# Hybrid attention and delta-rule layer: the gate row's partition sum from a high and a low part, and new orders for all five queues

## The reference

```python
mod = silu(c) @ ada_w[l] + ada_b[l]
shift, scale, gate = split(mod, 3)
h = rmsnorm(x, pre_norm_w) * (1 + scale) + shift
proj = h @ w_in[l]
o_moba = moba_attention(mq, mk, mv) * silu(mg)      # one block of 256: causal softmax
o_dn = rmsnorm(gated_delta_rule(dq, dk, dv, g, beta), dn_norm_w) * silu(dz)
y = concat([o_moba, o_dn]) @ w_out[l]
x = x + gate * rmsnorm(y, post_norm_w)
```

## Time and profile before

| | us |
|---|---|
| median of 3 runs (200.59 to 201.94) | 201.45 |
| the profiled execution's own time | 201.38 |
| its span, first to last instruction | 199.2 |
| TensorE busy in it | 185.7 |
| VectorE, ScalarE, GpSimd busy | 138.4, 104.1, 83.4 |
| transfers | 38.43 MB, mean 193 GB/s |

### The profile page before, as it was taken

One profiled execution on the slowest core, in us unless ns is written; L12 is line 12 of the kernel. 1 busy time (PEld: TensorE's weight loads), 2 busy tenths in 40 slices (PEclk: granted clock), 3 DMA queues, 4 the chain that ended last, 5 costly groups with the idle time before them and its releaser, 6 DMA issues.

```text
span 199.2 us, 4716 instructions
## 1 busy us (share of the span) xinstructions
PE 185.7 (93%) x1898; PEld 170.3 (86%) x1898; DVE 138.4 (69%) x326; ACT 104.1 (52%) x201; POOL 83.4 (42%) x46
## 2 busy tenths in 40 slices
PE   7999779999999989999999999997999999899970
PEld 6897769999999989988989999896999987588850
DVE  0638989463079988979878646746989399837364
ACT  2835445636398869396553226385234548337230
POOL 2037709795969616928065003974000220504000
PEclk9988999999999999999999999999999999999998
DMA  5999999999106530197308400062029357910022
GB/s 211 394 403 404 409 396 407 400 406 408 42 0 207 175 147 0 44 396 305 105 3 273 151 3 3 3 212 106 3 74 412 151 205 223 359 59 0 3 107 105
DMA packets 11527, 38.43 MB, mean 193 GB/s; under 512 B 1393, under 2 KB 1521, under 8 KB 10994
## 3 DMA queue, kind: packets, MB, share of 16 engines
q1 hardware_dynamic: 11362, 37.61, 50.6%
q10 hardware_dynamic: 144, 0.52, 0.7%
HBM read 37.08 MB, written 1.05 MB: 191 GB/s over the span
## 4 chain that ended last, share of the span: by engine, by line
PE 51%; DVE 28%; DMA 8%; ACT 6%; issue 3%; POOL 1%; DVEq 0%; SPq 0%; ACTq 0%; POOLq 0%
PE bank L1337 11%; PE bank L1338 10%; PE bank L1339 10%; DVE cv L951 7%; DVE accg L1139 5%; DMA raw<-in_w_out 4%; PE bank L1348 4%; DVE bank L926 3%; DMA outb<-in_post_norm_w 3%; PE bank L1547 3%; PE bank L1558 3%; PE bank L1535 2%; DVE pr L1114 2%; ACT whi L544 1%; DVE ssq L1003 1%
## 5 line engine op out<-in xcount | busy, mean ns | idle before, releaser
L471 POOL TENSOR_TENSOR wlo<-raw,whi 128x1024 fp32r<-128x1024 f32 (+1 forms) x25 | 57.4, 2317 | 66.7 <-ACT whi L544 66.7
L1337 PE MATMUL bank<-hhi,whi 128*128 128x256 f32 x224 | 65.3, 292 | 3.0 <-DVE hlo L895 2.1
L1338 PE MATMUL bank<-hhi,wlo 128*128 128x256 f32 x224 | 63.6, 284 | 0.0
L1339 PE MATMUL bank<-hlo,whi 128*128 128x256 f32 x224 | 63.5, 283 | 0.0
L1337 PEld LDWEIGHTS bank<-hhi,whi 128*128 128x128 f32 x224 | 43.1, 193 | 5.2 <-DVE hlo L895 2.9
L1338 PEld LDWEIGHTS bank<-hhi,wlo 128*128 128x128 f32 x224 | 43.2, 193 | 0.0
L1339 PEld LDWEIGHTS bank<-hlo,whi 128*128 128x128 f32 x224 | 43.1, 193 | 0.0
L544 ACT ACTIVATE whi<-raw 128x1024 fp32r<-128x1024 f32 (+1 forms) x33 | 33.0, 1026 | 10.6 <-PE bank L1339 7.5
L951 DVE SCALAR_TENSOR_TENSOR cv<-bank,convh,cv 128x255 f32<-128x255 f32 (+2 forms) x36 | 17.0, 481 | 8.6 <-ACT cv L608 7.6
L926 DVE SCALAR_TENSOR_TENSOR bank<-ada,sml,bank 128x512 f32<-128x512 f32 (+1 forms) x24 | 16.5, 687 | 0.7
L485 POOL TENSOR_TENSOR rot<-rot,cst 128x512 f32<-128x512 f32 x4 | 4.4, 1091 | 22.3 <-DVE rot L1081 20.4
(11 more groups left out here) (203 smaller groups left out, 359.0 us busy)
## 6 DMA issues: line engine op xcount, KB each, us to landing
raw<-in_w_rest SPq DMA_DIRECT2D x20, 512.0 KB, 5.1
ada<-in_ada SPq DMA_DIRECT2D x12, 512.0 KB, 8.7
ada<-in_gate_w SPq DMA_DIRECT2D x4, 1024.0 KB, 8.3
raw<-in_w_out SPq DMA_DIRECT2D x8, 512.0 KB, 6.2
ada<-in_ada SPq DMA_DIRECT2D x8, 256.0 KB, 6.1
raw<-in_w_qkv SPq DMA_DIRECT2D x5, 384.0 KB, 7.7
qkvs<-in_w_qkv SPq DMA_DIRECT2D x4, 384.0 KB, 9.2
cv<-in_w_qkv SPq DMA_DIRECT2D x4, 384.0 KB, 13.6
```

The lines of the kernel that those rows point to most:

```text
L471: pool.tensor_tensor(split_u(wlo, n), raw_u(n), split_u(whi, n).bitcast(F32), ALU.subtract).then_inc(lo_done, 1)
L1337: pe.matmul(out, a[0][ia], b[0][ib], start=start, stop=False, skip_group_check=skip)
L1338: pe.matmul(out, a[1][ia], b[0][ib], start=False, stop=False, skip_group_check=skip)
L1339: return pe.matmul(out, a[0][ia], b[1][ib], start=False, stop=stop, skip_group_check=skip)
```

## The change

Four things. `gate_sum` multiplies rounded parts in place of float32: ScalarE rounds the ones (once) and a half of `accg` to `g_hi` (`gate_hi`), VectorE forms `g_lo = accg - g_hi` (`gate_lo`), and TensorE adds two products of 512 columns. The parts lie over `rot`, so `gate_hi(0)` waits for the last `rope`, and `gate_hi(1)` for `gate_sum(0)`. Of the low parts of the weights, units 34, 35, 37, 38 and 41 go from VectorE to GpSimd, and 28 from GpSimd to VectorE. And the lists of calls of all five queues stand in another order.

```diff
-        DVE_LO = (21, 34, 35, 37, 38, 41, 42, 43)
+        DVE_LO = (21, 28, 42, 43)
...
+            def gate_hi(i):
+                act.wait_ge(gate_acc, NK * (i + 1))
+                if i == 0:
+                    act.wait_ge(rope_done, 4)
+                    act.activation(g_ones, ones[:, :], ACT.Copy)
+                else:
+                    act.wait_ge(gate_ready, 1)
+                act.activation(g_hi, accg[:, i * 512:(i + 1) * 512], ACT.Copy).then_inc(gate_hi_done, 1)
...
+            def gate_lo(i):
+                dve.wait_ge(gate_hi_done, i + 1)
+                dve.tensor_tensor(g_lo, accg[:, i * 512:(i + 1) * 512], g_hi.bitcast(F32), ALU.subtract).then_inc(gate_split, 1)
...
             def gate_sum(i):
-                pe.wait_ge(gate_acc, NK * (i + 1))
+                pe.wait_ge(gate_split, i + 1)
...
-                pe.matmul(bank[6][:, :], ones[:, :], accg[:, i * 512:(i + 1) * 512], start=True, stop=True).then_inc(gate_ready, 1)
+                pe.matmul(bank[6][:, :], g_ones, g_hi, start=True, stop=False)
+                pe.matmul(bank[6][:, :], g_ones, g_lo, start=False, stop=True).then_inc(gate_ready, 1)
...
+            load_gates()
             load_front()
             load_ada(0, 0, 2)
             load_ada(0, 2, 4)
+            load_gate_bias()
             load_unit(0)
-            load_ada(1, 2, 4)
+            load_unit(1)
             load_ada(1, 0, 2)
             load_unit(2)
-            load_unit(1)
+            load_ada(1, 2, 4)
...
             qkv_products(8)
+            mod(4)
             qkv_products(9)
-            mod(4)
...
             scores(1)
-            half(10)
-            half(11)
             t_turn(1, 0)
+            t_turn(1, 1)
             z_products(1, 0)
-            t_turn(1, 1)
```

More of the change, by code:

```diff
@@ L143, in build @@
         sb("hold_qkvs", [P, NQKV * S + 1024])
-        rot = sb("rot", [P, 3, 512])
+        with ExitStack() as e:
+            rot = sb("rot", [P, 3, 512], into=e)
+        with ExitStack() as e:
+            gsplit = sb("gsplit", [P, 3, 512], F32R, into=e)
+        sb("hold_rot", [P, 3 * 512])
         pr, pT = sb("pr", [P, 2, 384]), sb("pT", [P, 2, 384])
@@ L1233, in _ @@
             gates_in()
-            rope(0)
             conv_silu(0)
             conv_silu(1)
+            rope(0)
             gates_out()
@@ L1262, in _ @@
             gated_heads(0)
+            v_tokens(1)
             mask_z(0, 0)
-            maxima(1)
-            v_tokens(1)
             mask_z(0, 1)
-            rope(2)
-            normalise(1)
             mask_z(1, 0)
@@ L1271, in _ @@
             merge(1, 0)
-            q_decayed(0)
+            rope(2)
             merge(1, 1)
+            maxima(1)
             mask_z(2, 0)
@@ L1277, in _ @@
             merge(2, 1)
+            mask_z(3, 0)
+            lo(28)
             q_decayed(1)
-            mask_z(3, 0)
+            normalise(1)
             merge(3, 0)
@@ L1285, in _ @@
             rope(3)
-            heads_lo(0)
+            gate_sums(0, 0, 4)
             mask_z(4, 1)
             mask_z(5, 0)
-            gated_heads(1)
             merge(4, 1)
             merge(5, 0)
+            gated_heads(1)
+            mask_z(5, 1)
             maxima(2)
+            gate_sums(0, 4, 8)
+            heads_lo(0)
             normalise(2)
-            heads_lo(1)
-            mask_z(5, 1)
-            lo(34)
+            gate_sums(1, 0, 4)
             merge(5, 1)
-            gate_sums(0, 0, 4)
-            gate_sums(0, 4, 8)
             gate(1)
+            gate(2)
             gated_heads(2)
-            lo(35)
             state_update(0)
             maxima(3)
-            gate_sums(1, 0, 4)
+            gate_sums(1, 4, 8)
             normalise(3)
-            heads_lo(2)
-            gate(2)
             state_update(1)
             gate(3)
-            gate_sums(1, 4, 8)
+            gate_lo(0)
+            o_sums(0)
             state_update(2)
-            o_sums(0)
+            o_scale(0)
+            heads_lo(1)
+            heads_lo(2)
             gated_heads(3)
-            o_scale(0)
-            lo(37)
-            lo(38)
+            gate_rows(0)
+            gate_lo(1)
             o_sums(1)
-            gate_rows(0)
+            gate_rows(1)
+            heads_lo(3)
             o_scale(1)
-            heads_lo(3)
             o_gate(0)
             o_gate(1)
-            gate_rows(1)
             dn_lo(0)
-            lo(41)
+            dn_lo(1)
             lo(42)
             lo(43)
-            dn_lo(1)
             finish(0)
@@ L1764, in _ @@
             half(7)
+            rows(0)
             scores(0)
-            rows(0)
             half(8)
@@ L1786, in _ @@
             x_products(1, 1)
+            t_turn(2, 0)
             z_products(2, 0)
-            t_turn(2, 0)
+            half(10)
             t_turn(2, 1)
@@ L1792, in _ @@
             x_products(2, 1)
-            t_turn(3, 0)
             z_products(3, 0)
             z_products(3, 1)
+            t_turn(3, 0)
+            half(11)
             x_products(3, 0)
@@ L1802, in _ @@
             t_turn(4, 1)
+            p_turn(1)
             t_turn(5, 0)
@@ L1805, in _ @@
             z_products(5, 0)
-            p_turn(1)
+            pv(1)
             half(12)
-            pv(1)
             x_products(4, 1)
             x_products(5, 0)
+            z_products(5, 1)
+            t_turn(5, 1)
             scores(2)
@@ L1814, in _ @@
             half(14)
-            p_turn(2)
-            t_turn(5, 1)
-            z_products(5, 1)
-            u_products(0)
-            x_products(5, 1)
-            pv(2)
-            w_products(1)
             half(15)
             half(16)
+            half(17)
+            x_products(5, 1)
+            u_products(0)
+            p_turn(2)
+            w_products(1)
+            pv(2)
             state_products(0)
             scores(3)
-            half(17)
+            half(18)
             vnew_products(1)
-            half(18)
             half(19)
             state_products(1)
+            p_turn(3)
             qk_products(0)
```

161 lines of the change are left out of this document (83 added, 78 removed).

## The result

The changed kernel takes 205.59 us (median of 4 runs, 205.31 to 207.54), the kernel before beside it 201.14 (4 runs, 200.59 to 201.94). The ratio is 1.024, with a 95% interval of 1.016 to 1.031: slower by about 4.5 us, and 2.2 above the range that was forecast. Medians here are of all runs; the ratios leave out runs of over 1.5% above the fastest of the same kernel. The profiled execution took 205.31 us, its span is 203.2, 4.0 more than before.

What follows compares the result with a forecast made beforehand. The prediction took TensorE's work and waits, plus what lies before its first and after its last product, as the bound. Terms -0.9 - 0.3 - 1.2 + 1.3 + 0.6 = -0.5 against 201.38 gave 200.9 us, range 198.6 to 203.4.

Steps and rivals of the forecast that it cites:

- the inverse's levels: half(10) and half(11) move out of the first level's front; hand-over gaps and normalise(1) perhaps caught: +0.6 us, ends 0.1 and 2.7.
- the thin cover: First level of the inverse, no half covering hand-overs: four gaps of 0.05 to 0.15 us, 0.3 in sum.
- the chance of the collision: normalise(1) may be caught by lo(29), making merge(3,0) late and t_turn(4,0) wait 0.4 us, taken at even chances.
- Gate sum, -0.9: Two rounded products replace one float32 product on TensorE, saving 0.47 us twice; subtractions and roundings lie beside other work.
- Wait before the second gate sum, -0.3: The 0.5 us wait for gate_rows(0) goes, gate_lo(1) arrives about 0.2 late: -0.3 us together; ends -0.5 and +0.7.
- `p_turn(2)`, -1.2: Five halves (14.4 us) now stand ahead, covering VectorE's 11.3 us chain, so TensorE's wait goes: -1.2 us.
- `p_turn(3)`, +1.3: Reached earlier, while lo(36) on GpSimd catches normalise(3) after its first multiplication: 8.2 against 7.0 us; ends 0 and 1.8.
- The front, 0: load_gates and load_gate_bias go first, 0.43 us issue each, covered by TensorE's dummy products and turns of x: zero, else +0.4.
- The clock in the earlier trace: TensorE's granted clock before the change was read as full in all slices but three of the first four and the last.
- 10% by way of the gate sums: Third rival: lo(35) reaches into gate_sums(1, 4, 8) and all behind moves, up to 2.4 us: +1.9, 203.3 us, chance 10%.
- the rivals: No new wait, 198.9 us (26%); gate's low parts caught, 204.3 (9%); gate sums caught, 203.3 (10%); transfers late, 202.2 (7%).
- Those with a collision: Rivals where GpSimd's low parts hold VectorE: gate_lo subtractions caught, 204.3 us (9%); gate sums caught, 203.3 us (10%).

Runs made afterwards that it cites:

- The kernel with the three edits: Changed kernel with load_gates behind load_unit(4), normalise(1) ahead of q_decayed(1) and lo(28), merge(5,1) ahead of gate_sums(1,0,4): 199.62 us, ratio 0.993.
- 6 dummies: Gate weights later, normalise(1) first and merge ahead, with 6 dummy products of TensorE ahead of mod_direct(2) in place of 8: 199.25 us (5 runs).
- that edit alone in the kernel before: Kernel before with only load_gates (gate weights, 32 KB in 128 packets) moved ahead of load_front: 202.26 us, ratio 1.005.

## Why the prediction was wrong

The step that failed is that of the inverse's levels: "At even chances with rounding up: +0.6 us; ends 0.1 and 2.7, one full low part on top". It cost 5.1. Three things were mis-sized there or left out.

- *How many low parts.* I saw that `normalise(1)` may be caught by `lo(29)` and stopped there. `hi(29)` and `hi(30)` stand next to each other on ScalarE, so GpSimd has two low parts without a gap, and an operation of VectorE that missed the first start waits for both (4.82 us). The bound had to be two: 2.4 more than mine. The wait of TensorE was 2.54 where I wrote 0.4.
- *What follows a wait.* I counted waits as their own length; the sum has no term for the clock. A wait of 2.5 us brought 1.5 us of half clock here, and 2.8 and 3.4 in two other traces.
- *The gate sums beside it.* `gate_sums(0, 0, 4)` took 5.13 us beside `lo(31)`, and `x_products(4, 1)` waited 0.33 for it. VectorE and GpSimd in the changed kernel:

```profile
128.25 5.13 DVE L1161 SCALAR_TENSOR_TENSOR accg<-ada,sml,accg 128x512 f32<-128x512 f32 x4
```

```profile
130.18 2.65 POOL L477 TENSOR_TENSOR wlo<-raw,whi 128x1024 fp32r<-128x1024 f32 x1 [2.64 <-ACT whi L554]
```

What is left of the 5.1, about 0.7, is the thinner cover. The kernel with the three edits confirms it, since its levels aren't caught: it ends 1.64 us before the kernel before; `half(8)` accounts for -0.6, the gates for -0.7 and -0.5, `p_turn(2)` for -1.2 and `scores(3)` for +0.7, so the levels cost +0.7. Of my 0.6, only 0.3 stood for the thin cover and the rest for the chance of the collision; so the cover was mis-sized too, by 0.4, and that the two numbers lie near each other means nothing.

The other steps:

- **Gate sum, -0.9**: -0.75 measured. Its two subtractions took 0.69 us each and were hidden.
- **Wait before the second gate sum, -0.3**: -0.5; `gate_lo(1)` was in time.
- **`p_turn(2)`, -1.2**: as forecast. No run undid this step alone.
- **`p_turn(3)`, +1.3**: 0 in the changed kernel's trace, 0.7 in four of the eleven other traces of this order. The mechanism is as forecast, a race; its margin is a few hundredths of a microsecond, so that it was won here is chance, and kept the total 0.7 us nearer to the forecast. The size was 0.7, since state and products ahead of it took longer than I had summed.
- **The front, 0** ("If that cover is gone, +0.4"): +1.2, of which the profiled executions put +1.8 on the gate weights, which I judged by 0.43 us of issue and not by what they do to the transfer behind them; the rest of the front became 0.6 shorter (waits for low parts of h: 1.4 for 2.1) and hid a third of it. By medians the gate weights cost 1.0 to 1.3 us.
- **The clock in the earlier trace rows.** I read three low slices among the first four; there are two, both 8.
- **The page.** I gave the rule of the Trainium skill, SBUF: State Buffer, section "Who interferes with whom", 10% by way of the gate sums. The trace agrees with it: gate sums of 3.11 us took 5.13 and 9.39 beside low parts. The section also says that whichever instruction starts first has the shared ports and the other stands still for all of it; 0.24 against 2.39 us for the same four columns, and 1.01 against 3.17 for `normalise(3)`, show just that here.

Of the rivals none was the one that came. Those with a collision took it one low part at a time.

The change is not all bad. With the gate weights behind unit 4, `normalise(1)` first and the merge ahead, it beats the kernel before by 1.7 us (0.993), with 6 dummies by 2.0 (0.991, interval 0.988 to 0.994). The two intervals overlap.

## What to carry to other kernels

When an engine's work moves beside another engine's that can hold it up, look for runs of neighbours in the other's queue, and bound the loss by the whole run of them, not by one piece; then add the slower clock behind a wait. What is placed first in a queue of loads is judged by when the load behind it lands, not by its bytes. Steps that others wait for (`normalise`, `merge`) go ahead of fillers (`lo`, gate sums) wherever both are ready.

## What was unexpected in the hardware

- A VectorE operation on 128x4 elements took 2.39 us beside a low part on GpSimd, and 0.24 when it started 0.17 us before one. Operations with one operand in a PSUM bank were not held: the first of `maxima(2)` took 0.30 us at 130.39, inside `lo(31)` (from 129.43).
- It works both ways: `lo(29)` took 2.97 us, not 2.4, where `lo(28)` on VectorE had started before it.
- With 32 KB in 128 packets at the head of the queue VectorE starts on the 512 KB behind them at 7.61 us, not 6.61, and at 8.05 with that edit alone in the kernel before; 0.46 of it is the later issue. Behind x they delayed the next pieces by 0.3 and 0.7.
- TensorE's clock fell to its lower level after idle times of 1.4, 1.5, 2.5 and 3.0 us; behind the 1.23 us of the earlier trace rows the page of before shows it full. In front a gap of 0.21 us went with as low a clock as one of 1.19 (0.66 from 10 to 20 us).
- The price of one and the same wait of 2.5 us differed by 1.9 us from trace to trace (1.5, 2.8 and 3.4 us of half clock behind it).
